# Decoder layer: norm taken behind the projection, chunk order, dots and early loads moved, additions per tile

## The chip, the cores and the metric

The kernel runs on one core of one Trainium2 chip. The metric is the time of one execution in device microseconds; where several runs are made, their median counts.

## The reference

One layer of a decoder. 16 meta tokens and 512 tokens of 1024 numbers are normed and projected by one matrix to queries, keys and values of two attentions (a differential one, and one over 128 keys that an indexer picks), the indexer's own queries and keys, and two gates. Both outputs are projected, gated, added and projected again. Then a feed-forward part picks 128 of 16384 single-neuron experts for each token by product keys, 16 for each of 8 heads.

```
xn = rms_norm(h, mix_norm_gain)
proj = xn @ w_in
aq, ak, av, bq, bk, bv, iq, ik, iw, gate_a, gate_b = split(proj)
aq, ak = rope(rms_norm(aq)), rope(rms_norm(ak))
...
mixed = sigmoid(gate_a) * y_a + sigmoid(gate_b) * y_b
h = h + mixed @ w_out
hn = rms_norm(h, ffn_norm_gain)
...
act = gelu(einsum('thkd,td->thk', u[expert], hn))
h = h + einsum('thk,thkd->td', g * act, v[expert])
```

`rms_norm(x, gain)` is `x * rsqrt(mean(x*x) + eps) * gain`.

## The kernel before, in words

All order is written out by hand: each engine has its own program, and semaphores join them. The engines are PE (matrix products), DVE, ACT and POOL (elementwise work) and SP, which issues most DMAs. Products of full fp32 precision are made of three fp32r products: a matrix is split into a high part (a cast, by ACT) and a low part (the difference, by POOL or DVE), and high x high, high x low and low x high are summed in PSUM.

**Projection** (`project`, lines 203 to 676). x comes in four tiles of 128 tokens, the meta tokens in a fifth of 16 rows. `CHUNKS` (line 62) lists ten chunks of output columns: `ak`, `small` (bk, bv, ik, iw: 200 columns), `av`, `aq`, four gate chunks, `iq`, `bq`, each of 512 columns but for `small`. A chunk is two pieces of four blocks of 128 rows of the weights; a slot is one piece for one token tile, 12 products. So slots 0 to 4 are `ak`'s first piece for tiles 0 to 4, slots 5 to 9 its second. Before that PE transposes each tile (`turn_x`, L616), DVE multiplies the bank by the norm's gain (L386), ACT takes the high part (L530), DVE the low part (L375). The sum of squares of x (L512), its root (L516), the inverse (L196 to L200) and the scaling of x (L369) stand ahead of it. ACT splits the weights (L524) and POOL subtracts (L345); POOL fills `ident`, `tri` and three key tiles at the start (L331 to L341).

The query and key chunks then are normed by head and rotated: ACT squares the bank (L575), DVE reduces it, ACT takes the root (L579), DVE inverts it and rotates in the bank (L484, L415 to L418), PE turns the result (L629), ACT copies it out. A bank is used again six steps (chunk and tile) later, and PE waits for its rotation. DVE builds the rotation tables with the gains and the lambda first (L398 to L409), and ACT's exp for the lambda (L534) stands ahead of its split of the third piece.

**Attention and routing** (`mix_and_route`) follows to about 740 us, and then the **experts' first half**: for each of 128 columns (expert index modulo 128), PE multiplies 128 rows of u, split by ACT (L1319, `uh`) and POOL (L1401, `ul`), by three token tiles (L1161 to L1163); ACT applies GELU (L1326) and SP stores the result to `act_mat` (L951). SP loads u four columns ahead (L947). The fourth token tile (number 3, `GATHERED`) goes another way: its 128 picked rows of u are gathered one a time by POOL (L1409), and DVE makes a dot product of each with the tile (L1586). The columns are staged: in three **turn** stages of 16 columns (30 to 45, 64 to 79, 98 to 113) PE multiplies half a column and then four one-hot matrices of four tokens (L1187) that DVE builds (L1685, L1688), in 32 groups, to lay out the gates; between them are **gaps** (46 to 63, 80 to 97), in which the gates of the tile before are stored (L958), and behind them the **tail** (114 to 127). `dot_plan` lays the 128 dots into these places, `GATHER_AT` each gather two columns behind the dot that frees its buffer.

```
        if i == 3:
            plan += [("gap", i, j, 2 * STARTS[i] + j * 2 * AHEAD[i] // GAP_DOTS) for j in range(GAP_DOTS)]
        plan += [("turn", i, g, 2 * TURNS_AT[i] + g // 2) for g in range(TURNS * TURN_GROUPS) if g % 8 != 7]
```

**The v stage** (`experts`): for each column, gates times activations (L1904) is split (ACT L1895, DVE L1909), v is split (ACT L1878 or L1893, DVE L1906), and PE adds up 18 products for three token tiles in six banks (L1864). SP loads v, gates and activations in pairs of columns; `load_early` issues those of pair 0 and part of pair 1 behind column 124. DVE adds the gathered rows of v for tile 3 (L1922, gathers by POOL L1844). At the end DVE adds the banks to the stream, tile by tile (L1929), and SP stores it (L1834).

Of the kernel before, what the change touches and what calls it, by code (L numbers as in the profile page):

```python
# [61 lines left out]
CHUNKS = ["ak", "small", "av", "aq", "gate", "iq", "gate", "bq", "gate", "gate"]  # L62
# [141 lines left out]
def project(nc, m, d):  # L204
# [6 lines left out]

    xn = placer(nc, m.free2)("xn", [P, 2, D])
# [31 lines left out]
    ms = gap("ms", [P, 8])  # L244

# [11 lines left out]
    xn_ready = nc.alloc_semaphore("xn_ready")  # L257
    xn_turned = nc.alloc_semaphore("xn_turned")
# [17 lines left out]
    N_PIECES = PIECES * len(CHUNKS)  # L276

# [21 lines left out]
    with nc.Block() as block:  # L299
        @block.sync  # L300
        def _(sp):
# [8 lines left out]
            load_weights(0)  # L310
            load_weights(1)
# [17 lines left out]
        def _(pool):  # L329
# [12 lines left out]
            for n in range(N_PIECES):  # L342
                w = width_of(n)
                pool.wait_ge(w_high, n + 1)
                nc.gpsimd.tensor_tensor(wlo[:, n % 3, :, 0:w], wraw[:, n % 3, :, 0:w], whi[n % 2][:, :, 0:w].bitcast(F32),  # L345
                                        ALU.subtract).then_inc(w_low, 1)

        @block.vector
        def _(dve):
# [9 lines left out]
            dve.wait_ge(squared, NT + 1)  # L359
            nc.vector.tensor_scalar(ms[:, 0:NT + 1], sums[:, 0:NT + 1], 1.0 / D, EPS, ALU.mult, ALU.add).then_inc(ms_ready, 1)  # L360
            dve.wait_ge(root_ready, 1)
            inverse_root(nc, step, inv[:, 0:NT + 1], root[:, 0:NT + 1], ms[:, 0:NT + 1])

            def normed(i):
                r = rows_of(i)
                src = m.stream[:, i, :] if i < NT else meta[:]
                if i >= 2:
                    dve.wait_ge(xn_turned, i - 1)
                nc.vector.tensor_scalar(xn[0:r, i % 2], src, inv[0:r, i:i + 1], None, ALU.mult).then_inc(xn_ready, 1)  # L369

# [6 lines left out]
            normed(0)  # L377
            normed(1)
            dve.wait_ge(mix_loaded, 16)
            for i in range(NT + 1):  # L380
                r = rows_of(i)
                dve.wait_ge(xn_turned, i + 1)
# [4 lines left out]
                if i + 2 <= NT:  # L387
                    normed(i + 2)
                dve.wait_ge(gained_x, i + 1)
                low_of(i)  # L390


# [47 lines left out]
            for q, n in enumerate(ROT_STEPS):  # L440
# [12 lines left out]
                if kind == "small":  # L453
# [13 lines left out]
                    if i < NT:  # L467
                        nc.vector.tensor_scalar(m.iw[:, i], x[:, 3 * HEAD:SMALL], IDX_HEADS ** -0.5 * HEAD ** -0.5,
                                                None, ALU.mult)
# [1570 lines left out]
```

## Time and profile before

| | us |
|---|---|
| median of 3 runs | 1881.32 (1880.59 to 1883.3) |
| profiled execution, its own time | 1884.28 |
| its span, first to last instruction | 1882.5 |
| PE busy | 1778.0 (94%) |
| PE weight loads, beside the products | 1483.5 (79%) |
| DVE busy | 1344.6 (71%) |
| ACT busy | 721.2 (38%) |
| POOL busy | 660.8 (35%) |
| mean granted clock of PE | 0.967 |

A busy time is the time in which an engine has an instruction in work. The span holds all instructions of the program; the time of an execution holds some 2 us more. The granted clock is 1.00 at 2.4 GHz and 0.50 at 1.2 GHz. The page cuts the span in 40 slices of 47 us, and gives in tenths how busy each engine is in each; where PE's digit is 9 and its clock is not, or the other way round, is where to look.

### The profile page before, as it was taken

The page shows a single profiled execution, that of the slowest core. Times are in us where ns is not written, and L with a number is a line of the kernel's source. Part 1 is how long each engine was busy: PE and PEld are TensorE (multiplying, and loading weights), DVE is VectorE, ACT ScalarE, POOL GpSimd, SP SyncE. Part 2 cuts the span into 40 slices and gives each one's busy share as a digit, 9 for nine tenths or more (in the row PEclk, how much of TensorE's full clock was granted, in tenths as well). Part 3 has the DMA queues.
Part 4 walks back from the last instruction along what each step waited for, and adds up shares of the span by engine and source line. Part 5 has one row for each costly group of instructions (what it writes and reads, how often), then busy time and mean ns, then how long its engine had stood idle before and what let it go on. Part 6 is the DMA issues. An engine that isn't in the chain of part 4 may idle for free.

```text
span 1882.5 us, 24827 instructions
## 1 busy us (share of the span) xinstructions
PE 1778.0 (94%) x8763; PEld 1483.5 (79%) x8767; DVE 1344.6 (71%) x2706; ACT 721.2 (38%) x1201; POOL 660.8 (35%) x416
## 2 busy tenths in 40 slices
PE   5899998999878989999989998999899999999998
PEld 4788875554555678999989998999788888888886
DVE  6843268465546877979979953992588888888886
ACT  4333334141222232355435533553343343343342
POOL 3234320000000332677676777776322222222220
PEclk9899997999898999999989999999899999999999
DMA  3222202434242662588887899886999999899993
GB/s 126 68 84 95 91 30 105 158 110 152 96 155 90 206 201 84 163 294 282 281 325 261 286 360 406 309 284 208 362 361 334 327 333 333 328 333 332 328 333 118
DMA packets 170192, 429.78 MB, mean 228 GB/s; under 512 B 15328, under 2 KB 66144, under 8 KB 165744
## 3 DMA queue, kind: packets, MB, share of 16 engines
q1 hardware_dynamic: 133056, 294.23, 45.4%
q0 software_dynamic: 36864, 134.23, 19.3%
q8 instruction: 55, 0.90, 0.2%
q14 instruction: 41, 0.34, 0.0%
q10 hardware_dynamic: 176, 0.07, 0.0%
HBM read 384.44 MB, written 44.04 MB: 228 GB/s over the span
## 4 chain that ended last, share of the span: by engine, by line
PE 73%; DVE 6%; DMA 3%; ACT 1%; issue 1%; POOL 1%; DVEq 0%; ACTq 0%
PE psum L1864 28%; PE psum L1161 8%; PE psum L1162 8%; PE psum L1163 8%; PE psum L1103 6%; PE psum L1187 5%; PE psum L1090 3%; PE psum L1011 3%; DMA u<-in_u 2%; PE psum L1059 1%; POOL ul L1401 1%; PE psum L1142 1%; DMA act_mat<-act_w 1%; DVE nmax L1460 1%; DVE hits L1615 1%
## 5 line engine op out<-in xcount | busy, mean ns | idle before, releaser
L1401 POOL TENSOR_TENSOR ul<-u,uh 128x1024 fp32r<-128x1024 f32 x128 | 321.8, 2515 | 532.3 <-ACT uh L1319 531.0
L1161 PE MATMUL psum<-split,uh 128*128 128x384 f32 x1024 | 357.0, 349 | 13.8 <-POOL ul L1401 13.8
L1163 PE MATMUL psum<-split,ul 128*128 128x384 f32 x1024 | 345.1, 337 | 0.0
L1162 PE MATMUL psum<-split,uh 128*128 128x384 f32 x1024 | 345.1, 337 | 0.0
L1844 POOL DMA_INDIRECT v_row<-in_v,gv x128 | 122.3, 956 | 383.5 <-DVE psum L1922 369.9
L1864 PE MATMUL psum<-vl,wh 128*128 128x512 f32 x768 | 240.9, 395 | 0.0
L1161 PEld LDWEIGHTS psum<-split,uh 128*128 128x128 f32 x1024 | 194.6, 190 | 18.0 <-POOL ul L1401 16.3
L1162 PEld LDWEIGHTS psum<-split,uh 128*128 128x128 f32 x1024 | 194.6, 190 | 1.4 <-issue 1.4
L1163 PEld LDWEIGHTS psum<-split,ul 128*128 128x128 f32 x1024 | 194.1, 190 | 0.0
L1864 PEld LDWEIGHTS psum<-vl,wh 128*128 128x128 f32 x768 | 144.9, 189 | 33.9
L1922 DVE SCALAR_TENSOR_TENSOR psum<-v_row,w,psum 128x1024 f32<-128x1024 f32 x127 | 162.8, 1282 | 0.0
L1319 ACT CAST uh<-u 128x1024 fp32r<-128x1024 f32 x128 | 133.6, 1045 | 74.6 <-DMA u<-in_u 74.5
L1326 ACT ACTIVATE act_w<-psum 128x384 f32<-128x384 f32 x128 | 62.9, 491 | 242.6 <-PE psum L1163 231.1
L1891 ACT COPY gate<-stage 128x128 f32 (+1 forms) x126 | 37.6, 299 | 298.8 <-PE psum L1864 286.9
L345 POOL TENSOR_TENSOR wlo<-wraw,whi 128x2048 fp32r<-128x2048 f32 (+1 forms) x20 | 87.3, 4363 | 165.5 <-ACT whi L524 165.5
L658 PE MATMUL psum<-whi,xTh 128*128 128x512 f32 (+1 forms) x344 | 135.6, 394 | 8.7 <-DVE rot L418 4.0
L1904 DVE TENSOR_TENSOR gate<-gate,act_v 128x384 f32<-128x384 f32 x128 | 73.4, 574 | 88.1 <-ACT gate L1877 46.1
L1685 DVE TENSOR_TENSOR hot<-iota,psum 128x1024 f32<-128x1024 f32 x96 | 116.8, 1217 | 26.1 <-PE psum L1175 25.4
L660 PE MATMUL psum<-whi,xTl 128*128 128x512 f32 (+1 forms) x344 | 133.3, 388 | 0.0
L659 PE MATMUL psum<-wlo,xTh 128*128 128x512 f32 (+1 forms) x344 | 132.9, 386 | 0.0
L1586 DVE SCALAR_TENSOR_TENSOR rows_sb<-rows_sb,psum 128x1024 f32<-128x1024 f32 x86 | 103.8, 1215 | 37.7 <-DMA rows_sb<-in_u_rows,tri 37.7
L1864 PE MATMUL psum<-vh_first,wh 128*128 128x512 f32 x384 | 121.9, 398 | 6.7 <-DVE wl L1909 6.7
(291 smaller groups left out, 3376.0 us busy)
## 6 DMA issues: line engine op xcount, KB each, us to landing
u<-in_u SPq DMA_DIRECT2D x128, 512.0 KB, 5.0
v<-in_v SPq DMA_DIRECT2D x64, 1024.0 KB, 5.0
act_mat<-act_w SPq DMA_DIRECT2D x128, 192.0 KB, 5.1
act_v<-act_mat SPq DMA_DIRECT2D x64, 384.0 KB, 6.7
wraw<-in_w_wide SPq DMA_DIRECT2D x18, 1024.0 KB, 5.1
gate_mat<-stage SPq DMA_DIRECT2D x16, 1024.0 KB, 10.1
gate<-gate_mat SPq DMA_DIRECT2D x128, 128.0 KB, 6.1
w_low<-in_w_branch_b SPq DMA_DIRECT2D x8, 1024.0 KB, 5.2
```

The costliest lines, as they stand in the source:

```text
L658: nc.tensor.matmul(ps, xh, wh, start=(part == 0 and k == 0), stop=False)
L659: nc.tensor.matmul(ps, xh, wl, start=False, stop=False)
L660: last = nc.tensor.matmul(ps, xl, wh, start=False, stop=(part == PIECES - 1 and k == PK - 1))
L1161: nc.tensor.matmul(out, high[:, c], split[:, 0:DENSE, 0, c], start=(c == 0), stop=False)
L1162: nc.tensor.matmul(out, high[:, c], split[:, 0:DENSE, 1, c], start=False, stop=False)
L1163: last = nc.tensor.matmul(out, low[:, c], split[:, 0:DENSE, 0, c], start=False, stop=(c == DC - 1))
L1319: nc.scalar.copy(uh[:, n % UH_COLS], u[:, n % U_COLS]).then_inc(s["u_high"], 1)
L1401: nc.gpsimd.tensor_tensor(ul[:, n % U_COLS], u[:, n % U_COLS], uh[:, n % UH_COLS].bitcast(F32), ALU.subtract).then_inc(s["u_low"], 1)
L1685: nc.vector.tensor_tensor(hot[:, b], keys, bcast(turned[:, 0:2, some], 3, N_KEYS), ALU.is_equal).then_inc(s["hot_rows"], 1)
L1844: nc.gpsimd.indirect_dma_start(out=rows_sb[k % V_RING][:], out_offset=None, in_=d.v.rearrange("j i n -> (j i) n"), in_offset=bass.Indirect ...
L1864: mm = nc.tensor.matmul(bank(m, 2 * i + half), lhs, rhs[:, half * 512:(half + 1) * 512], start=first and k == 0 and p == 0, stop=last and ...
L1922: nc.vector.scalar_tensor_tensor(mixed0, rows_sb[n % V_RING][:], m.w0[:, n:n + 1], mixed0, ALU.mult, ALU.add).then_inc(s["mixed"], 1)
```

## The change

The parts, in the order of the program:

- `CHUNKS` has `av` second and `small` third.
- x is transposed and split as it comes (`turn_x` reads the stream, `xn` is gone). The inverse norm of each token, `inv_x`, is worked out behind the split of x, and multiplies the products where they leave PSUM (as `scale` of ACT's instruction, or of a copy), the inverse of each head's norm for the rotated chunks (a new DVE instruction in `head_scale`), and `iw`.
- SP issues x tile 0, the first weights, x tiles 1 and 2, the second weights, x tile 3.
- The first weights are split in two halves; PE waits for each. ACT splits the second weights after the second x tile, POOL's three key memsets stand behind the first weights.
- `GAP_DOTS` is 14 instead of 28; all 32 groups of a turn stage have a dot; the tail has 10 instead of 8.
- `load_early` becomes `load_first` (pair 0, behind column 116) and `load_second` (v and activations of pair 1, behind column 120).
- On ACT the cast of the first `wh` and the GELU of the dots stand ahead of the last two columns.
- PE signals each token tile of the last column by itself, and DVE adds it then.

```diff
-CHUNKS = ["ak", "small", "av", "aq", "gate", "iq", "gate", "bq", "gate", "gate"]
+CHUNKS = ["ak", "av", "small", "aq", "gate", "iq", "gate", "bq", "gate", "gate"]
...
             for i in range(NT):
                 sp.dma_start(m.stream[:, i, :], d.x[i * P:(i + 1) * P, :]).then_inc(x_loaded[i], 16)
-            load_weights(0)
-            load_weights(1)
+                if i in (0, 2):
+                    load_weights(i // 2)
...
-            nc.gpsimd.memset(m.akT[:], 0.0)
-            nc.gpsimd.memset(m.bkT[:], 0.0)
-            nc.gpsimd.memset(m.ikT[:], 0.0).then_inc(keys_zeroed, 1)
             for n in range(N_PIECES):
+                if n == 1:
+                    nc.gpsimd.memset(m.akT[:], 0.0)
...
-                pool.wait_ge(w_high, n + 1)
...
+                for k, chunks in enumerate(HALVES if n == 0 else (slice(0, PK),)):
+                    pool.wait_ge(w_high, parts_before(n) + k + 1)
...
-            def normed(i):
...
-                nc.vector.tensor_scalar(xn[0:r, i % 2], src, inv[0:r, i:i + 1], None, ALU.mult).then_inc(xn_ready, 1)
...
                 low_of(i)
 
+            dve.wait_ge(squared, NT + 1)
+            nc.vector.tensor_scalar(ms_x[:, 0:NT + 1], sums[:, 0:NT + 1], 1.0 / D, EPS, ALU.mult, ALU.add).then_inc(ms_ready, 1)
+            dve.wait_ge(root_ready, 1)
+            inverse_root(nc, step, inv_x[:, 0:NT + 1], root_x[:, 0:NT + 1], ms_x[:, 0:NT + 1])
+            nc.vector.tensor_copy(ms_x[:, 0:NT + 1], inv_x[:, 0:NT + 1]).then_inc(x_inverse, 1)
...
+                if heads == GROUPS:
+                    step(nc.vector.tensor_scalar(inv[0:r, 0:heads], inv[0:r, 0:heads], inv_x[0:r, i:i + 1], None, ALU.mult))
...
+            act.wait_ge(dve_order, 1)
+            split_weights(0)
+            high_of(0)
+            high_of(1)
+            split_weights(1)
+            squares_of(0)
+            squares_of(1)
+            high_of(2)
+            squares_of(2)
+            squares_of(3)
+            high_of(3)
+            squares_of(NT)
+            high_of(NT)
...
                     if q == 0:
                         act.wait_ge(x_low, NT + 1)
+                        act.wait_ge(x_inverse, 1)
...
-                        nc.scalar.activation(raw[0:r, q % 2], ps, ACT.Square).then_inc(evacuated, 1)
+                        nc.scalar.activation(raw[0:r, q % 2], ps, ACT.Square, scale=inv_x[0:r, i:i + 1]
+                                             ).then_inc(evacuated, 1)
...
-                    nc.scalar.copy(m.av[0:r, i], ps).then_inc(evacuated, 1)
+                    nc.scalar.mul(m.av[0:r, i], ps, inv_x[0:r, i:i + 1]).then_inc(evacuated, 1)
...
             def turn_x(i):
...
-                pe.wait_ge(xn_ready, i + 1)
+                pe.wait_ge(x_loaded[i], 16)
...
-                                               xn[0:r, i % 2, c * P:(c + 1) * P], m.ident[0:r, 0:r])
...
+                                               src[:, c * P:(c + 1) * P], m.ident[0:r, 0:r])
...
-                    if i == 0:
-                        pe.wait_ge(w_low, piece + 1)
+                    if i == 0 and slot > 0:
+                        pe.wait_ge(w_low, parts_before(piece) + 1)
...
+                        if slot == 0 and k % (PK // 2) == 0:
+                            pe.wait_ge(w_low, 2 * k // PK + 1)
...
-GAP_DOTS = 28
+GAP_DOTS = 14
...
-        plan += [("turn", i, g, 2 * TURNS_AT[i] + g // 2) for g in range(TURNS * TURN_GROUPS) if g % 8 != 7]
+        plan += [("turn", i, g, 2 * TURNS_AT[i] + g // 2) for g in range(TURNS * TURN_GROUPS)]
...
-                if n == N_KEYS - U_COLS:
-                    late.load_early(sp)
+                if n == 2 * TAIL_AT + 2:
+                    late.load_first(sp)
+                if n == 2 * TAIL_AT + 6:
+                    late.load_second(sp)
...
             late.high_of_v(act, 1)
-            alone(PAIRS - 1, PAIRS)
+            late.high_of_w(act, 0)
             act.wait_ge(s["dotted"], PICKS)
             nc.scalar.activation(dots[:], dots[:], ACT.Gelu).then_inc(s["act0_ready"], 1)
+            alone(PAIRS - 1, PAIRS)
             late.high_parts(act)
...
         load_pair(sp, 0, 0)
+
+    def load_second(sp):
         load_v(sp, 2, 1)
         load_activated(sp, 2, 1)
...
-                mm.then_inc(s["summed"], 1)
+                    if last and k == RING - 1:
+                        mm.then_inc(s["tile_summed"], 1)
+                if not last or k < RING - 1:
+                    mm.then_inc(s["summed"], 1)
...
+    def high_of_w(act, n):
+        act.wait_ge(s["gated"], n + 1)
+        nc.scalar.copy(wh[n][:], gate[n // 2][:, n % 2]).then_inc(s["w_high"], 1)
...
-        dve.wait_ge(s["summed"], N_KEYS)
         for i in range(DENSE):
+            dve.wait_ge(s["tile_summed"], i + 1)
             nc.vector.tensor_tensor(m.stream[:, i, :], m.stream[:, i, :], bank(m, 2 * i, 2),
                                     ALU.add).then_inc(s["added"], 1)
```

**Order.** The first instructions of ACT that work (raw and part are scratch, `whi` the weights' high part, `xTh` that of x). Before:

```order
L512 ACT_TABLE_LOAD
L512 ACTIVATE raw,sums<-meta 16x1024
L512 ACTIVATE raw,sums<-stream 128x1024 x4
L516 ACT_TABLE_LOAD
L516 ACTIVATE root<-ms 128x5
L524 CAST whi_71<-wraw 128x2048
L530 CAST xTh<-raw 128x8x128
L530 CAST xTh<-rot 128x8x128
L530 CAST xTh<-raw 128x8x128
```

And now:

```order
L514 ACT_TABLE_LOAD
L514 CAST whi_71<-wraw 128x1024 x2
L519 CAST xTh<-raw 128x8x128
L519 CAST xTh<-rot 128x8x128
L514 CAST whi_72<-wraw 128x2048
L525 ACTIVATE part,sums<-stream 128x1024 x2
L519 CAST xTh<-raw 128x8x128
L525 ACTIVATE part,sums<-stream 128x1024 x2
L519 CAST xTh<-rot 128x8x128
L525 ACTIVATE part,sums<-meta 16x1024
L519 CAST xTh<-raw 128x8x16
L544 ACT_TABLE_LOAD
```

The squares have moved from ahead of all to between the casts of x, and the second weights stand between tiles 1 and 2.

POOL behind its constants (`wlo` is the weights' low part, `akT`, `bkT` and `ikT` the key tiles). Before:

```order
L338 IOTA iota_i 128x128
L339 MEMSET akT 128x4224
L340 MEMSET bkT 128x1056
L341 MEMSET ikT 128x1056
L345 TENSOR_TENSOR wlo<-wraw,whi_71 128x2048
L345 TENSOR_TENSOR wlo<-wraw,whi_73 128x2048
L345 TENSOR_TENSOR wlo<-wraw,whi_71 128x4x200
```

And now:

```order
L345 IOTA iota_i 128x128
L354 TENSOR_TENSOR wlo<-wraw,whi_71 128x1024 x2
L348 MEMSET akT 128x4224
L349 MEMSET bkT 128x1056
L350 MEMSET ikT 128x1056
L354 TENSOR_TENSOR wlo<-wraw,whi_72 128x2048
L354 TENSOR_TENSOR wlo<-wraw,whi_71 128x2048
```

The memsets stand between the first and the second weights, and the third piece is wide.

SP behind column 116 of the experts' first half, as it is now (L967 loads u, L971 stores activations, L1815 to L1822 load the v stage's first pairs):

```order
L971 DMA act_mat<-act_w 128x384
L1815 DMA v_2622<-in_v 128x2x1024
L1819 DMA gate_2632<-gate_mat 128x2x128 x2
L1822 DMA act_v_2640<-act_mat 128x768
L967 DMA u<-in_u 128x1024
...
L971 DMA act_mat<-act_w 128x384
L1815 DMA v_2623<-in_v 128x2x1024
L1822 DMA act_v_2641<-act_mat 128x768
L967 DMA u<-in_u 128x1024
```

Before, both portions stood together behind column 124:

```order
L951 DMA act_mat<-act_w 128x384 x2
L1792 DMA v_2596<-in_v 128x2x1024
L1796 DMA gate_2606<-gate_mat 128x2x128 x2
L1799 DMA act_v_2614<-act_mat 128x768
L1792 DMA v_2597<-in_v 128x2x1024
L1799 DMA act_v_2615<-act_mat 128x768
L951 DMA act_mat<-act_w 128x384 x3
```

The loads have left the last stores' neighbourhood; the gates of pair 1 stay behind the last column in both.

## Rows read from the trace of the kernel before

**Rows 1.** Waits of PE, 0 to 250 us: us in all, times, longest.
```profile
PE psum L629 <- DVE rot L472: 4.7, 2, 2.6
PE psum L658 <- DVE rot L418: 4.0, 2, 2.4
```

**Rows 2.** DMA issues at 0.7 and 2.7 us: size, us to landing.
```profile
stream<-in_x SPq DMA_DIRECT2D x1, 512.0 KB, 4.3
...
wraw<-in_w_wide SPq DMA_DIRECT2D x1, 1024.0 KB, 8.6
```

**Rows 3.** Timeline: start, duration (us), engine, line, instruction; idle before it.
```profile
2.44 3.61 POOL L339 MEMSET akT<- 128x4224 f32 x1
2.60 3.53 DVE L354 CAST ident_b<-ident 128x128 bf16<-128x128 f32 x1 [1.71 <-POOL iota_i L338]
4.40 1.28 ACT L512 ACT_TABLE_LOAD   x1 [4.40 <-DMA meta<-in_meta_tokens]
13.25 1.88 ACT L524 CAST whi<-wraw 128x2048 fp32r<-128x2048 f32 x1
18.55 1.05 ACT L530 CAST xTh<-raw 128x1024 fp32r<-128x1024 f32 x1 [3.42 <-DVE raw L386]
20.66 1.21 DVE L375 TENSOR_TENSOR xTl<-raw,xTh 128x1024 fp32r<-128x1024 f32 x1
22.02 0.47 PE L658 MATMUL psum<-whi,xTh 128*128 128x512 f32 x1 [3.14 <-DVE xTl L375]
```

**Rows 4.** Windows: PE, PEld, DVE, ACT, POOL busy (count), clock, DMA, GB/s; then timeline.
```profile
42.00:56.00 14.00, 13.88 (x60) 11.28 (x61) 11.43 (x36) 3.63 (x7) 1.98 (x2) 1.00 0.09 28
63.60:66.90 3.30, 3.30 (x15) 3.30 (x16) 2.76 (x9) 1.84 (x4) 0.00 (x0) 0.50 0.02 5
...
37.39 4.68 POOL L345 TENSOR_TENSOR wlo<-wraw,whi 128x2048 fp32r<-128x2048 f32 x1 [17.20 <-ACT whi L524]
37.56 4.70 DVE L401 TENSOR_TENSOR sin_ak<-sin,gains 128x160 f32<-128x160 f32 x1
52.26 0.69 DVE L433 TENSOR_REDUCE ms<-raw 128x8 f32<-128x512 f32 x1
56.72 0.69 DVE L418 TENSOR_TENSOR rot<-psum,part 128x512 f32<-128x512 f32 x1
115.31 0.39 PE L658 MATMUL psum<-whi,xTh 128*128 128x512 f32 x1
```

**Rows 5.** Windows of the third gap and of the tail.
```profile
1093.00:1180.00 87.00, 79.90 (x434) 77.69 (x433) 30.05 (x50) 26.27 (x35) 66.00 (x44) 0.96 1.01 396
1276.00:1334.00 58.00, 58.00 (x336) 57.79 (x334) 7.20 (x12) 20.65 (x30) 35.40 (x19) 1.00 0.69 223
```

**Rows 6.** Second turn stage: window, two DVE rows, a row of the chain.
```profile
1000.00:1092.00 92.00, 92.00 (x619) 91.60 (x618) 90.71 (x123) 54.20 (x61) 65.33 (x45) 1.00 0.86 280
...
1046.09 0.08 DVE L1586 DVE_READ_ACCUMULATOR rows_sb<-rows_sb,psum 128x1 f32 x1
1049.08 0.08 DVE L1586 DVE_READ_ACCUMULATOR rows_sb<-rows_sb,psum 128x1 f32 x1
1044.49 0.89 PE psum L1187 x8
```

**Rows 7.** Before the v stage: chain, timeline of SP, PE, ACT, window after.
```profile
1326.35 12.59 DMA act_mat<-act_w
1339.90 0.95 SPq L1796 DMA_DIRECT2D gate<-gate_mat  x2
1340.84 0.77 PE L1864 MATMUL psum<-vh_first,wh 128*128 128x512 f32 x1 [6.72 <-DVE wl L1909]
1346.65 0.30 ACT L1891 COPY gate<-stage 128x128 f32<-128x128 f32 x1 [3.43 <-DMA gate<-gate_mat]
...
1340.00:1347.00 7.00, 6.16 (x15) 4.84 (x16) 5.31 (x7) 0.96 (x4) 1.94 (x2) 0.50 1.04 405
```

**Rows 8.** Timeline of the end, DVE.
```profile
1875.77 3.48 DVE L1929 TENSOR_TENSOR stream<-stream,psum 128x1024 f32<-128x1024 f32 x3 [11.20 <-PE psum L1864]
```

More of the change, by code:

```diff
@@ L276, in project, with parts_before @@
     N_PIECES = PIECES * len(CHUNKS)
+    SQUARED = (0, 1, 2, 3, NT)
+    HALVES = (slice(0, PK // 2), slice(PK // 2, PK))
+    def parts_before(piece):
+        return piece + (piece > 0)
     def width_of(piece):
@@ L428, in rotate, with head_scale @@
                 return nc.vector.tensor_tensor(out, a, b, ALU.add)
-            def head_scale(sq, heads, k):
+            def head_scale(sq, heads, k, i):
                 r = sq.shape[0]
@@ L505, in _ @@
             act.dma_start(m.mix_gain[:], d.mix_gain).then_inc(mix_loaded, 16)
-            act.wait_ge(dve_order, 1)
-            for k, i in enumerate([NT] + list(range(NT))):
-                r = rows_of(i)
-                act.wait_ge(x_loaded[i], 16)
-                src = m.stream[:, i, :] if i < NT else meta[:]
-                nc.scalar.activation(raw[0:r].rearrange("p a b -> p (a b)"), src, ACT.Square,
-                                     accum_out=sums[0:r, i:i + 1]).then_inc(squared, 1)
-                act.wait_ge(squared, k + 1)
-            act.wait_ge(ms_ready, 1)
-            nc.scalar.activation(root[:, 0:NT + 1], ms[:, 0:NT + 1], ACT.Sqrt).then_inc(root_ready, 1)
             def split_weights(n):
@@ L523, in split_weights, with high_of @@
                 w = width_of(n)
-                nc.scalar.copy(whi[n % 2][:, :, 0:w], wraw[:, n % 3, :, 0:w]).then_inc(w_high, 1)
-            split_weights(0)
-            for i in range(NT + 1):
+                for chunks in HALVES if n == 0 else (slice(0, PK),):
+                    nc.scalar.copy(whi[n % 2][:, chunks, 0:w], wraw[:, n % 3, chunks, 0:w]).then_inc(w_high, 1)
+            def high_of(i):
                 lo = columns_of(i)
@@ L1779, in experts @@
     gathered = [nc.alloc_semaphore(f"v_gathered{k}") for k in range(V_RING)]
[L1780 removed]
+    names = "v_high v_low gate_kept gated w_high w_low summed tile_summed mixed added stored".split()
     s = s | {n: nc.alloc_semaphore(n) for n in names}
@@ L1893, in body @@
                     nc.scalar.copy(vh[k % HIGH_RING], v[k // 2][:, k % 2]).then_inc(s["v_high"], 1)
-                act.wait_ge(s["gated"], n + 1)
-                nc.scalar.copy(wh[k % HIGH_RING][:], gate[k // 2][:, k % 2]).then_inc(s["w_high"], 1)
+                if not first or k >= 1:
+                    act.wait_ge(s["gated"], n + 1)
+                    nc.scalar.copy(wh[k % HIGH_RING][:], gate[k // 2][:, k % 2]).then_inc(s["w_high"], 1)
         rounds(act, body)
```

66 lines of the change are left out of this document (35 added, 31 removed).

## Prediction

> **What bounds the kernel now.** I read the page first (which engine is busy in which slice), then the waits of PE, and then, for each stretch in which PE waits, the timeline, the windows with the granted clock, and the chain of waits. PE is busy for 94% of the span and heads the chain, so two things alone are worth anything: time in which PE stands still, and time in which it runs at 1.2 instead of 2.4 GHz after it stood still. Other engines' work beside a busy PE is priced at nothing.
>
> In the projection PE's first product starts at 22.02 us [rows 3]. Behind it PE waits 4.0 us for banks that DVE must rotate first and 4.7 us at the turns of the narrow chunk [rows 1]; such a wait is often followed by a stretch at clock 0.50 [rows 4]. In the third gap (columns 80 to 97) PE is busy 79.90 of 87.00 us while the DMA engines are at 1.01 of their time [rows 5]. Before the v stage PE stands for 6.72 us, and the 7 us that follow go at clock 0.50 [rows 7]. At the end DVE adds three tiles one after the other [rows 8]. The rest of PE's idle time lies in the attention stage, which is not touched.
>
> **Start of the projection.** The norm leaves the path: the squares, a root, the inverse and the scaling of x. The first x tile lands 4.3 us after an issue at about 0.8, so at 5.1; the first weights land 8.6 us after an issue at about 2.6, at 11.2, behind four x tiles [rows 2]. So 2560 KB came in 6.1 us, 2.4 us for 1024 KB. In the new order the weights come behind one tile: 5.1 + 2.4 = 7.5. ACT then loads its table (1.28) and casts the weights in halves (1.88 in all): 9.8 and 10.8. Only then comes the high part of x (1.05): 11.8 [rows 3]. POOL subtracts the first half meanwhile (half of 4.68, to 12.3). DVE's low part of x (1.21) has both inputs in SBUF and cannot run beside that: such an instruction of 128x160 took 4.70 us where POOL subtracted for 4.68 [rows 3, 4]. That gives 13.5 for PE's first product, 8.5 us earlier.
>
> The lead is not kept whole. Each tile passes DVE (gain, of the same width as the low part: 1.2), ACT 1.05, DVE 1.21 in series, 4 us with the hand-overs, against 2.8 us of products (60 matmuls in 14.00 us, 12 a slot) and a turn [rows 3, 4]; and ACT now has the second weights (1.88) and the squares between these casts. POOL does its memsets behind the first weights (to about 21) and then the second weights, which holds DVE's low part of tile 2 until 26. I get product slots 1, 2 and 3 at 19.5, 27 and 31, and slot 5 (second weights) at about 36.6 where it was 42.1. The ends are 32.4 (tile 2 gets in ahead of POOL) and 38.
>
> The low part of tile 1 meets a memset. The nearest row has a CAST of 128 columns held for 3.53 us beside a memset of 3.61 [rows 3], so I take it as held: slot 1 a microsecond later, and tile 2 sure to be behind POOL's subtraction. The Trainium skill (SBUF — State Buffer, "Who interferes with whom") says that a DVE instruction with two SBUF inputs contends with a GpSimd instruction that reads SBUF, not with one that only writes it. By it this memset holds nothing, tile 2 comes to its low part at 21.8 with POOL's subtraction due at 21.3, and the early end of 32.4 is half a microsecond away; the sum would then be up to 4 us better. No run shows the case yet.
>
> **Chunk order.** Rotating one ak tile takes DVE from 52.26 to 57.41, 5.2 us [rows 4], plus one new instruction of 0.2: 5.4. After ak came the narrow chunk, whose slots take 1.1 to 1.4 us, and PE caught up with DVE; now ten av slots of 2.8 us come first. The rotations start no earlier than tables and lambda: x is split at 31.5, root and inverse take 3, the tables 5 (estimates from the widths), and then the third weights, wide now, hold DVE behind POOL until 46.5. The first rotation is done at 51, the next at 56.6, 63 (once more behind POOL), 68.7 and 74; PE wants the first at 50.5, the third at 60 and the fourth at 66 and waits 0.6, 3 and 2.4 us. Later the narrow chunk's first rotation meets POOL's subtraction for aq (4.6 us) and PE waits 4 us at its turn. So 10 us of waits stand where 8.7 stood: they move, they do not go. With two or three slow stretches (each 3.4 us at half rate, 1.7 lost), the first aq product comes at about 107.5 instead of 115.3 [rows 4], and four small turns (0.5) are still to come: **7 us** for the whole stage, between 3 and 12. After that the order is as before and DVE has time, so the gain is kept.
>
> **Dots.** In the third gap 18 columns want 18 x 704 KB (u tile and store), eight gate stores of 1024 KB and 28 gathers of 512 KB: 36.0 MB, 91 us at the row's 396 GB/s; the stretch took 87 [rows 5]. The floor is PE's: 14 tail columns took 58.00 us, 4.14 each [rows 5], so 75 us for 18. With 14 gathers it is 28.7 MB or 72.5 us, just under the floor. In the 16 columns with stores the demand is 397 GB/s, right at what the row delivers, so I leave 2 us of waits: 87 - 75 - 2 = **10 us**, between 6 and 12. The removed dots go into turn groups that had none (12) and into the tail (2). A group with a dot takes DVE 2.99 us; it takes PE half a column (2.07) and the eight small products (0.89), 2.96 [rows 5, 6]. Groups without a dot let DVE catch up. Some 72 of the 96 groups by 0.03: **2 us** lost (the first eight groups of each turn have dots from the start and already go at DVE's pace), between 0 and 3. The tail's dots are done long before PE needs them.
>
> **Early loads of v.** The chain before the v stage is a store of act_mat that takes 12.59 us (it shares the DMA engines with 3072 KB of early loads and six gathers of v rows), ACT's last GELU, one cast and one subtraction [rows 7]. The loads now go out after columns 116 and 120, where DMA moves only 223 GB/s [rows 5]; behind the first of them the queue is longer by 1664 KB, 4.2 us, and u tiles are asked for four columns (16.6 us) ahead, so nothing waits there. The cast of w and the GELU of the dots stand ahead of the last pair, beside the last columns. Against gathers alone I take 6 to 7 us for the store (estimate), so it lands before the last column ends at 1334.1; then GELU 0.5 and PE starts at 1334.8 instead of 1340.84: 6.0 us. After so short a stop the clock should stay up; 6.1 us at 0.50 had cost 3.1. Late next are the gates of pair 1, still asked for only after the last column. They were asked for at 1339.90 and landed at 1346.65 [rows 7]; from 1335.1 they land at 1341.8, copy, split and product take 3 (estimate), and PE wants them at 1334.8 + 8.3 = 1343.1, so 1.5 is lost again: **7.6 us**, between 4 and 9.5.
>
> **End.** DVE's three additions (3.48 us from 1875.77) become one behind the last matmul (1.2) [rows 8]: **2.3 us**, give or take 0.2.
>
> **Sum.** 7 + 10 - 2 + 7.6 + 2.3 = 24.9. Against the profiled execution (span 1882.5, time 1884.28) that is 1857.6 and 1859.4. The median of the runs lies 3.0 below that execution, so **1856**. A measurement of this kernel tells about 0.2% (3.8 us) from no change.
>
> **Rivals.** *The projection stays bound by DVE.* POOL's subtractions hit the fourth and fifth rotation as well and the clock falls after each wait: the 7 shrinks to 1, 1862. For it: three of my waits are already conflicts of DVE and POOL. Against: PE starts 8.5 us sooner.
>
> *The gap stays full.* 397 GB/s are wanted where 396 came; u tiles go on coming late through eight stores, and 10 becomes 4: 1862. For it: DMA at 1.01 [rows 5]. Against: half of the gathers are gone.
>
> *Slower, by the dots in the turn groups.* DVE has no spare time left in 96 groups. If each dot waits d for its row, PE loses 96 d; from d = 0.26 the whole gain is gone, at 0.35 it is 1890. Against: with seven dots in eight groups DVE's instructions follow each other without a pause, and DMA is at 0.86 there [rows 6].
>
> *The early loads do not do what they say.* The six gathers (3 MB) are the store's real neighbours; if it still takes over 10 us, PE starts at 1337 or later and the clock drops: 7.6 becomes 3, 1860.5.
>
> *A better start.* No hold at the memset, and tile 2 ahead of POOL: 4 us more, 1852.
>
> **Chances.** Forecast, each term near its value: 0.50 (1850 to 1862 by itself). Projection alone poor 0.13, gap alone poor 0.12, early loads poor 0.08, better start 0.10, nothing left of the gain (several poor, within 3.8 us) 0.03, slower by the dots 0.04. The range of 1847 to 1866 leaves out the slow end and the sums of two poor cases. Faster by over 0.2%: 0.93, within 0.03, slower 0.04.
>
> **What would show it.** First product at 13 to 16 us, slot 5 at 33 to 38, the first aq product at 104 to 111, and DVE instructions of 3 to 5 us beside POOL's weight subtractions. In the gap 76 to 80 us for 18 columns; in the turns groups at 2.99. At the v stage one wait under 1.5 us and a clock that stays at 1.00, then a short wait at pair 1; one addition after the last matmul. I am wrong if the first aq product comes after 112, if the gap still takes over 83 us, or if the v stage starts more than 2 us after the last column.

## The result, and the profile after

| | before | after |
|---|---|---|
| median of the runs side by side | 1880.95 us (6 runs, 1876.89 to 1883.74) | 1865.89 us (6 runs, 1860.17 to 1871.45) |
| ratio | | 0.9912, 95% interval 0.9895 to 0.9929 |
| profiled execution, its own time | 1884.28 | 1860.17 |
| its span | 1882.5 | 1858.4 |
| PE busy | 1778.0 (94%) | 1769.8 (95%) |
| mean granted clock of PE | 0.967 | 0.976 |

The change is faster by 0.9%, 17 us by the ratio, where 24.9 were forecast (1856 us). The median lies within the range of 1847 to 1866, at its very end. The profiled execution is the fastest of the six; two more sets of runs of the same kernel (e1, e9) gave medians of 1860.07 and 1864.6 and ratios of 0.9883 and 0.9896, so the gain is about 19 us. That the profiled execution lies so near the forecast of 1859.4 for it is luck.

The start of the page: digits are tenths in each of 40 slices.

```profile
PE   7989998899878999999989999999899999999999
...
PEclk9999997999998999999999999999999999999999
```

Most of what is left of idle PE and low clock lies in the slices of the attention stage (7, 8 and 11 to 13 of the 40), as before; the rest is the start (slices 1 and 3), column 58 (slice 21) and the start of the v stage (slice 29). I read the stages from the timeline of PE: the start of the first product at slot 40 (the third slot of the first gate chunk), at columns 9, 80, 98 and 127 of the experts' first half, and at column 4 of the v stage. The times between these marks, in all profiled executions of this study:

| kernel | to slot 40 | to col. 9 | to 80 | gap, to 98 | to 127 | to v col. 4 | to the end |
|---|---|---|---|---|---|---|---|
| before | 143.5 | 570.2 | 379.0 | 87.4 | 149.7 | 30.5 | 522.1 |
| **after** | 138.0 | 564.7 | 380.5 | 75.6 | 150.6 | 29.3 | 519.6 |
| e1, change again | 139.3 | 564.1 | 380.3 | 76.5 | 150.5 | 26.6 | 519.6 |
| e2, gathers held | 140.3 | 569.7 | 379.8 | 76.0 | 151.4 | 21.7 | 520.9 |
| e3, low parts in four | 134.5 | 570.5 | 379.9 | 79.2 | 150.4 | 29.7 | 519.6 |
| e4, projection as before | 145.3 | 569.9 | 379.5 | 79.9 | 150.5 | 29.2 | 519.7 |
| e5, dots as before | 141.0 | 564.6 | 377.5 | 85.4 | 149.5 | 29.9 | 519.6 |
| e6, loads late | 139.1 | 560.9 | 380.1 | 75.9 | 150.2 | 30.8 | 519.6 |
| e7, narrow second | 139.0 | 570.2 | 380.1 | 75.8 | 150.2 | 29.5 | 519.6 |
| e8, three edits | 134.7 | 570.2 | 375.7 | 75.8 | 150.5 | 21.7 | 523.6 |
| e9, change a third time | 140.8 | 568.3 | 380.6 | 77.5 | 151.1 | 29.8 | 519.6 |
| e10, narrow second again | 138.7 | 567.4 | 379.7 | 76.0 | 150.3 | 29.6 | 519.6 |
| e11, six ahead | 134.9 | 570.4 | 375.7 | 76.1 | 150.3 | 22.2 | 519.6 |

The first two rows differ by 24.1 us: 5.5 in the projection, 5.5 in the attention stage, 11.8 in the gap, 1.2 at the v stage, 2.5 at the end, less 2.4 in turns, at column 58 and in the tail. None of the instructions of the attention stage was changed; how much of its 5.5 us the change brings all the same stays open (e1, e4, e7).

**The projection.** The waits of PE from 0 to 250 us, which answer to [rows 1]:

```profile
PE psum L634 <- DMA stream<-in_x: 7.1, 2, 5.4
PE psum L647 <- DVE rot L473: 6.6, 3, 4.2
PE psum L678 <- DVE xTl L372: 6.2, 2, 3.4
PE psum L678 <- DVE rot L417: 3.3, 2, 2.8
```

The timeline of POOL, DVE and PE in the projection, rows of the start (as [rows 3]) and of the narrow chunk:

```profile
13.78 0.79 PE L678 MATMUL psum<-whi,xTh 128*128 128x512 f32 x1 [2.73 <-DVE xTl L372]
15.90 3.62 POOL L348 MEMSET akT<- 128x4224 f32 x1
16.04 1.23 DVE L372 TENSOR_TENSOR xTl<-rot,xTh 128x1024 fp32r<-128x1024 f32 x1 [1.18 <-ACT xTh L519]
21.33 4.55 POOL L354 TENSOR_TENSOR wlo<-wraw,whi 128x2048 fp32r<-128x2048 f32 x1
22.43 4.53 DVE L372 TENSOR_TENSOR xTl<-raw,xTh 128x1024 fp32r<-128x1024 f32 x1 [1.24 <-ACT xTh L519]
...
94.60 4.57 POOL L354 TENSOR_TENSOR wlo<-wraw,whi 128x2048 fp32r<-128x2048 f32 x1 [5.82 <-ACT whi L514]
94.87 4.38 DVE L460 TENSOR_TENSOR part<-raw 128x64 f32<-128x64 f32 x1 [21.65 <-ACT raw L586]
106.33 4.49 DVE L424 TENSOR_TENSOR part<-raw,icos 128x32 f32<-128x32 f32 x1
120.24 4.54 DVE L467 COPY bv<-raw 128x64 f32<-128x64 f32 x1
```

PE starts at 13.78 instead of 22.02. The low part of tile 1 takes its 1.23 us beside the memset; that of tile 2 takes 4.53 us beside POOL's subtraction. The three last rows are small DVE instructions of the narrow chunk, each held while POOL splits a wide piece (at 94.60, 106.18 and 120.14); the first of them makes PE's wait of 4.2 us, which ends at 103.4, just ahead of the first aq product.

**The gap and the tail**, windows as in [rows 5]:

```profile
1083.00:1158.80 75.80, 75.66 (x438) 75.30 (x438) 17.13 (x30) 26.57 (x36) 57.42 (x33) 1.00 1.00 381
1254.90:1313.70 58.80, 58.76 (x339) 58.16 (x337) 17.46 (x29) 22.10 (x32) 42.02 (x24) 1.00 0.81 279
```

PE does not stop in the third gap any more, at 381 GB/s.

**The start of the v stage**: the chain of waits (as in [rows 7]), the timeline of ACT and DVE at pair 1, and the window around it:

```profile
1313.92 0.50 ACT act_w L1348
1314.81 0.43 SPq L1819
1315.29 9.88 DMA gate<-gate_mat
...
1325.19 0.30 ACT L1923 COPY gate<-stage 128x128 f32<-128x128 f32 x1 [10.38 <-DMA gate<-gate_mat]
1327.61 0.55 DVE L1942 TENSOR_TENSOR wl<-gate,wh 128x384 fp32r<-128x384 f32 x1
...
1323.00:1332.00 9.00, 3.78 (x10) 2.95 (x10) 6.09 (x8) 4.46 (x8) 1.00 (x1) 0.66 1.05 392
```

The first product comes at 1314.5, 5.1 us after column 127's instead of 11.0. Then the gates of pair 1, asked for at 1314.8, take till 1325.2, and PE stands 5.2 us at the second pair and comes back at the low clock. At the end DVE's additions follow PE tile by tile (the row holds all three), and the last product is 4.6 us from the end where it was 7.1 [rows 8]:

```profile
1851.42 3.94 DVE L1962 TENSOR_TENSOR stream<-stream,psum 128x1024 f32<-128x1024 f32 x3 [8.48 <-PE psum L1889]
```

### The profile page after: what moved, and what is told of

It reads as the page before. It is cut to its first block, busy times and chain, and to the rows that moved or that the text cites. A ratio compares the mean times of both kernels' runs of the same rounds, so it can differ in the third digit from the quotient of the medians.

```text
span 1858.4 us, 24842 instructions
## 1 busy us (share of the span) xinstructions
PE 1769.8 (95%) x8767; PEld 1472.3 (79%) x8767; DVE 1339.7 (72%) x2715; ACT 723.5 (39%) x1202; POOL 661.8 (36%) x417
## 4 chain that ended last, share of the span: by engine, by line
PE 76%; DVE 5%; DMA 1%; ACT 1%; issue 1%; POOL 1%; SPq 0%; DVEq 0%; ACTq 0%
PE psum L1889 28%; PE psum L1183 9%; PE psum L1185 9%; PE psum L1184 9%; PE psum L1125 6%; PE psum L1209 5%; PE psum L1112 3%; PE psum L1033 3%; PE psum L1081 2%; PE psum L1164 1%; PE psum L1059 1%; DVE nmax L1483 1%; DMA gate<-gate_mat 1%; DVE score L1455 1%; DMA u<-in_u 0%
## 5 line engine op out<-in xcount | busy, mean ns | idle before, releaser
L1183 PEld LDWEIGHTS psum<-split,uh 128*128 128x128 f32 x1024 | 193.7, 189 | 10.5 <-POOL ul L1424 8.8
L354 POOL TENSOR_TENSOR wlo<-wraw,whi 128x2048 fp32r<-128x2048 f32 (+2 forms) x21 | 87.7, 4180 | 160.1 <-ACT whi L514 160.1
L1708 DVE TENSOR_TENSOR hot<-iota,psum 128x1024 f32<-128x1024 f32 x96 | 116.9, 1217 | 36.6 <-PE psum L1197 36.6
L1364 ACT COPY stage<-psum 128x512 f32<-128x512 f32 x96 | 106.2, 1106 | 67.9 <-PE psum L1209 67.8
L1889 PE MATMUL psum<-vh_second,wh 128*128 128x512 f32 x384 | 120.5, 395 | 5.2 <-DVE wl L1942 5.2
```

Source lines behind the costliest of these rows:

```text
L1183: nc.tensor.matmul(out, high[:, c], split[:, 0:DENSE, 0, c], start=(c == 0), stop=False)
L1708: nc.vector.tensor_tensor(hot[:, b], keys, bcast(turned[:, 0:2, some], 3, N_KEYS), ALU.is_equal).then_inc(s["hot_rows"], 1)
L1889: mm = nc.tensor.matmul(bank(m, 2 * i + half), lhs, rhs[:, half * 512:(half + 1) * 512], start=first and k == 0 and p == 0, stop=last and ...
```

## The experiments

Each kernel was timed beside the kernel before on one chip; medians of different sets are compared by their ratios to it. e1 to e4 were timed together, so were e5 to e8, and e9 to e11.

**e1, the change again.** No edit.

> The changed kernel itself once more. Its profiled execution was 5.7 us below its median, and the attention stage (281 to 702 us), which the change does not touch, was 5.75 us shorter than before, with 68.3 us at granted clock 0.50 in it where the kernel before had 78.5. Theory A (the clock's stretches fall differently in every execution): attention takes anything from 421 to 433 us this time, and its time follows half of its half-clock time to within 1 us; projection (first aq product at 103 to 106), third gap (75 to 77 us) and first v product (within 1 us of the last column) repeat to within 1 us. Rival B (the change really shortens attention): attention takes 421 to 423 us again. Median 1863 to 1868 by both.

Median 1860.07 us (5 runs), ratio 0.9883 (0.9865 to 0.9901). Projection 1.3 us longer, gap and v start as expected, pair 1 came 1.8 us sooner (its v column 2 at 12.0 us behind the first product instead of 13.8). The attention stage gave the same 432 us as in the profiled execution of after, as rival B wants, and the median is 3 us below the 1863 to 1868 expected. What speaks against a B that gives the same gain each time are the others: after, e1, e2, e5, e6 and e9 have the same instructions up to column 9, and took 432.5, 431.9, 437.5, 432.5, 428.7 and 436.1 us (mean 433.2) from the projection's last slot to column 9; before took 438.3. That all six lie below it leaves room for a B on the average, to which e4 and e7 come back. The windows of after and of e2:

```profile
270.20:702.70 432.50, 385.64 (x1588) 246.98 (x1587) 281.26 (x889) 131.28 (x328) 31.26 (x12) 0.92 0.41 139
```

```profile
272.50:710.00 437.50, 394.73 (x1586) 251.81 (x1588) 284.56 (x891) 131.39 (x328) 31.91 (x12) 0.90 0.41 138
```

PE does the same work and is busy 9 us longer, at a mean clock of 0.90 instead of 0.92. The time does not simply follow the half-clock time as I had written: before and e2 had 78.5 and 88.7 us of it in 438.3 and 437.5 us. Where PE waits anyway, a slow stretch costs nothing.

**e2, gathers held.**

```diff
-            if k == V_RING - 2:
+            if k == V_RING - 4:
                 pool.wait_ge(s["hidden"], N_KEYS)
+                pool.wait_ge(loaded[1], LOADS)
```

> The change, but POOL issues 4 instead of 6 gathers of v rows ahead of the last column, and the next only when the v stage's second pair has landed. Theory (the gates of pair 1 took 9.9 us because the gathers had 78% of the DMA engines' time beside them): they land within 5 us of their issue, PE's 5.2 us wait at pair 1 falls to 1.5 or less and the 6.8 us at clock 0.50 behind it go: 6 to 8 us faster than the change, so 1858 to 1860. Rival (the gates are slow by themselves, 256 descriptors of 512 B behind the last stores): they take 8 us or more again, the wait stays over 3 us, and the time is within 2 us of the change.

The timeline of ACT at pair 1, and the use of the DMA queues while the gates were under way, in e2 (1322.5 to 1325.7 us):

```profile
1325.69 0.30 ACT L1924 COPY gate<-stage 128x128 f32<-128x128 f32 x1 [3.20 <-DMA gate<-gate_mat]
...
q1 hardware_dynamic: 758, 0.61, 73.0%
q0 software_dynamic: 30, 0.08, 6.1%
```

And in after, 1314 to 1320 us (q0 is POOL's queue with the gathers, q1 holds SP's transfers; the last number is the share of the DMA engines' time):

```profile
q0 software_dynamic: 525, 1.90, 78.1%
q1 hardware_dynamic: 558, 0.49, 23.7%
```

The gates, asked for at 1322.5, were there 3.2 us later instead of 10.4, and both the wait at pair 1 and the slow stretch are gone: 21.7 us from column 127 to v column 4, 7.6 less than after. The theory holds for the mechanism. In the time little of it is seen: median 1860.41 (4 runs), ratio 0.9865 (0.9850 to 0.9880) against 0.9883 and its interval of e1. The 6 to 8 us expected did not come. The trace gives 2.1 of the 7.6 us back, 0.8 in the tail and 1.3 in the rest of the v stage, where PE has a new wait of 1.0 us 26 us in.

**e3, low parts in four.**

```diff
-                for k, chunks in enumerate(HALVES if n == 0 else (slice(0, PK),)):
-                    pool.wait_ge(w_high, parts_before(n) + k + 1)
+                for k, chunks in enumerate(HALVES if n == 0 else QUARTERS):
+                    pool.wait_ge(w_high, parts_before(n) + (k if n == 0 else 0) + 1)
...
-                        pe.wait_ge(w_low, parts_before(piece) + 1)
+                        pe.wait_ge(w_low, lows_before(piece) + PK)
```

> The change, but POOL subtracts each piece of the weights but the first in four instructions of 128x512 instead of one of 128x2048. Theory (a DVE instruction with both inputs in SBUF is held until POOL's instruction ends, and gets in between two): the holds of 3.3 to 4.5 us on DVE become 1.2 us or less, PE's waits in the projection from 50 to 140 us shrink from 10.3 us to 3 to 5, one slow clock stretch less: slot 40 at 131 to 134 instead of 138.0, 4 to 7 us faster, 1859 to 1862. Rival (the hold lasts as long as POOL works, whatever the number of instructions): holds of 3 to 5 us stay and so does the time, within 2 us.

POOL's and DVE's timeline of e3, at the second weights, at the first ak rotation and at the narrow chunk:

```profile
20.90 6.00 POOL L359 TENSOR_TENSOR wlo<-wraw,whi 128x512 fp32r<-128x512 f32 x4
21.66 1.60 DVE L377 TENSOR_TENSOR xTl<-raw,xTh 128x1024 fp32r<-128x1024 f32 x1 [1.24 <-ACT xTh L524]
...
38.04 5.07 POOL L359 TENSOR_TENSOR wlo<-wraw,whi 128x512 fp32r<-128x512 f32 x4 [11.13 <-ACT whi L519]
39.36 1.26 DVE L438 TENSOR_SCALAR ms<-ms 128x8 f32<-128x8 f32 x1
41.91 1.22 DVE L198 TENSOR_TENSOR root<-root,ms 128x8 f32<-128x8 f32 x1
...
92.92 1.09 DVE L465 TENSOR_TENSOR part<-raw 128x64 f32<-128x64 f32 x1 [23.22 <-ACT raw L591]
```

A hold lasts until POOL's instruction ends: four short ones let DVE in between, at 5.07 us for POOL instead of 4.6. Of DVE's small instructions none takes more than 1.3 us any more, but now several in a row are held: at 103 to 108 us four take 1.18, 1.30, 1.17 and 1.21 us, where beside the whole piece one took 4.49. PE's waits from 50 to 140 us fell only from 10.3 to 8.4 us, not to 3 to 5. Most of the gain is at the start: the low part of tile 2 takes 1.60 us instead of 4.53, and slot 5 starts at 33.7 instead of 36.3. Slot 40 comes at 134.5, half a microsecond behind the band, 3.5 us sooner than in after and 5.2 sooner than the mean of the six executions of the whole-piece kernels (after, e1, e2, e5, e6, e9: 139.75).

The median, 1861.21 (ratio 0.9874, 0.9858 to 0.9889), can't tell it from e1: the gain of the projection is not in the time. In the profiled execution the attention stage, from the projection's last slot to column 9, took 438.5 us, 5.3 above the mean of the six. The same stage took 438.3 and 438.5 in e8 and e11, which have this projection too, each time with 81.9 us at granted clock 0.50. The gap took 79.2 us here, with a wait of 2.2 us and a slow stretch.

**e4, projection as before.** `project` and `CHUNKS` are those of the kernel before.

> The change with the projection of before (norm ahead of the products, narrow chunk second): dots, early loads and additions as in the change. By the two traces the projection's part is 5.2 us (slot 40 at 143.5 instead of 138.0), so this is 4 to 7 us slower than the change: 1870 to 1873. By rival B (attention gains through the projection as well) it is 10 to 12 slower: 1876 to 1878.

Median 1874.76, ratio 0.9939 (0.9925 to 0.9952). Beside e1 (0.9883), with which it was timed, that is 10.5 us slower by the ratios, as B says; against the other two sets of the change (0.9896 and 0.9912) it is 8 and 5 us. Slot 40 at 145.3 is 5.5 us behind the mean of 139.75, so more may be lost than the projection's own part. Its attention stage took 438.0 us, above all six of the change. The medians do not settle between the theory and B.

**e5, dots as before.** `GAP_DOTS = 28`, and `if g % 8 != 7` put back in `dot_plan`.

> The change with the dots as before (28 in the third gap, none in every eighth group, 8 in the tail). Theory (the third gap is bound by what the DMA engines deliver, and half of its gathers are half of its excess): columns 80 to 97 take 86 to 89 us instead of 76 to 80, a turn stage 0.6 us less, so 8 to 11 us slower than the change. Rival (the gap was slow in the execution before by luck of the clock): 80 to 83 us, 3 to 5 slower.

Median 1867.8, ratio 0.9925 (0.9905 to 0.9945). The window of columns 80 to 97:

```profile
1083.10:1168.50 85.40, 79.26 (x439) 76.48 (x437) 30.33 (x50) 26.30 (x35) 65.23 (x43) 0.98 1.01 400
```

The gap takes 85.4 us, 9.8 more than after, half a microsecond under the theory's band and above the rival's 80 to 83; the columns before it, with two turn stages and column 58, take 3.0 less (380.5 to 377.5), and those behind it, with the third, 1.1 less. Net that is about 6 us by the trace and 2 to 8 by the ratios, less than the 8 to 11 expected of the whole, since the turn stages give 1.7 us back and the stretch with column 58 took 2.1 us less in this execution. Moving the dots is worth this much.

**e6, loads late.** Both portions behind column 124 again, ACT's order as in the change.

> The change with both early portions of v behind column 124 again, the order on ACT as in the change. The forecast put 7.6 us on the early loads; the traces give 1.2 (30.5 to 29.3 us from column 127 to the first product of column 4) and 3.8 us in a second execution, because the gates of pair 1 come late in place of the last store. Theory (one wait took the place of the other): PE's first v product comes 9 to 11 us after column 127's first instead of 5.1, the wait at pair 1 is under 2 us, and the whole is 1 to 5 us slower than the change. Rival (the early loads are worth the 7.6 us forecast): 7 to 9 us slower.

Median 1862.72, ratio 0.9896 (0.9882 to 0.9911), the same as the change. The waits of PE, and the chain of waits:

```profile
PE psum L1888 <- ACT act_w L1347: 5.8, 1, 5.8
PE psum L1888 <- DVE wl L1941: 1.8, 1, 1.8
```

```profile
1302.80 12.89 DMA act_mat<-act_w
1317.13 8.37 DMA gate<-gate_mat
```

With the loads late the store takes 12.89 us and PE waits 5.8 us ahead of the first product and 1.8 at pair 1; with the loads early it waits 0.8 and 5.2. 30.8 us against 29.3, 26.6 and 29.8 for the change: one wait took the place of the other, as the theory says. The 1 to 5 us that it wanted in the time can't be seen in the medians. The rival, the forecast's own 7.6 us, falls.

**e7, narrow second, and e10, the same again.** `CHUNKS` as before.

> The change with the narrow chunk second again. Theory (av's ten wide slots hide some of DVE's rotations of ak, but most of it comes back at the narrow chunk's turns): slot 40 comes at 139 to 143 instead of 138 to 139.3, so 1 to 4 us slower than the change. Rival (the order only moves the waits): slot 40 within 1 us of the change's; a second rival (the order is worth the whole lead): slot 40 at 143 or later.

> e7 again beside the change. Its trace had slot 40 at 139.0 (the change 138.0 to 141.0), yet its median was 1869.0. Theory (the order of the chunks only moves waits; e7's slow attention stage of 438.3 us was the clock's luck): the profiled attention stage differs from e7's, slot 40 at 138 to 141, and the median is within 3 us of e9's. Rival (the order does more: it leaves attention in a state in which the clock falls oftener): attention 437 to 439 us again and a median 4 us or more above e9's.

Slot 40 came at 139.0 and 138.7, within the change's 138.0 to 141.0, so in the projection the order only moves the waits (in e7 4.5 us for banks and 3.5 at turns, in after 3.3 and 6.6). The attention stages were 438.3 and 435.5 us, so e7's was no fixed state. But both medians are high: they are 1869.03 (ratio 0.9925, 0.9912 to 0.9938) and 1868.35 (0.9928, 0.9915 to 0.9941), the second 3.8 us above e9's: more than the theory's 3 and less than the rival's 4. If the chunk order is worth some 3 to 5 us outside the projection, the traces show one place for them: the four executions with the narrow chunk second (before, e4, e7, e10) took 438.3, 438.0, 438.3 and 435.5 us in the attention stage, 437.5 on the average, against 433.2 of the six with av second. All these kernels run the same instructions there. Four and six executions that overlap do not prove it, and how the order would bear on a later stage is shown by nothing here.

**e8, three edits.** e2 and e3, and the gathers at column 58 spread:

```diff
-GATHER_AT = [FIRST_GATHERS] * U_RING + [min(DOTS[k][3] + 2, N_KEYS) for k in range(PICKS - U_RING)]
+GATHER_AT = [FIRST_GATHERS] * U_RING + [min(DOTS[k][3] + 2 + (DOTS[k][0] == "chosen") * max(DOTS[k][2] - 1, 0), N_KEYS)
+                                        for k in range(PICKS - U_RING)]
```

> The change with three edits: v gathers held until pair 1 has landed (e2), low parts of the weights in four instructions (e3), and the eight gathers that POOL issues in one go ahead of column 58 spread: two there, then one a column. Theory: slot 40 at 133 to 136, PE's wait of 7.6 us at column 58 under 2.5 and the clock stretch behind it gone (together 6 to 9 us), no wait at pair 1 (3 to 6 us): 1845 to 1851, against 1860 to 1866 of the change. Rival for the spread (the wait at column 58 comes from DVE's work on the picks beside POOL's subtractions, not from the gathers): it stays over 5 us.

Median 1853.41 (5 runs, 1851.51 to 1854.24), ratio 0.9841 (0.9829 to 0.9854). POOL's timeline at column 58, in after (the first and the last of eight gathers, then the late subtractions) and in e8:

```profile
943.74 0.95 POOL L1432 DMA_INDIRECT rows_sb<-in_u_rows,tri  x1
...
954.19 2.28 POOL L1432 DMA_INDIRECT rows_sb<-in_u_rows,tri  x1 [0.93 <-DVE rows_sb L1609]
956.49 11.10 POOL L1424 TENSOR_TENSOR ul<-u,uh 128x1024 fp32r<-128x1024 f32 x3
```

```profile
946.15 0.95 POOL L1438 DMA_INDIRECT rows_sb<-in_u_rows,tri  x1
947.41 0.94 POOL L1438 DMA_INDIRECT rows_sb<-in_u_rows,tri  x1 [0.30 <-issue]
948.37 2.40 POOL L1430 TENSOR_TENSOR ul<-u,uh 128x1024 fp32r<-128x1024 f32 x1
950.92 0.95 POOL L1438 DMA_INDIRECT abqT<-in_u_rows,tri  x1 [0.16 <-issue]
```

The wait of 7.6 us at column 58 and its slow stretch are gone; three waits for `ul` of 2.9 us in all and one of 1.9 for `hot` come later, and 4.8 us remain as gain (380.5 to 375.7). The time is 2.4 us above what I expected. In this execution the gathers held back in the v stage came with a wait of 2.2 us and a slow stretch of their own: 523.6 us from v column 4 to the end, 4 more than any kernel that gathers as the change does. That does not explain the median, since e11 is rid of both and no faster; the attention stage of 438.3 us, 5 above the mean of the change, may.

**e9, the change a third time.**

> The changed kernel a third time, beside e10 and e11 on one chip. Five profiled executions with the same instructions up to column 57 took 428.8 to 437.5 us from the end of the projection to column 9, by where the clock's slow stretches fell, so only medians of many runs compare kernels here. By both earlier sessions together: median 1860 to 1866, ratio to before 0.988 to 0.991.

Median 1864.6 (6 runs, 1856.3 to 1869.56), ratio 0.9896 (0.9877 to 0.9916), as expected. (In e5, one of the five executions named there, the dots already differ from column 33 on; the stretch that is compared ends at column 9 and is the same.) All 17 runs of the change lie between 1856.3 and 1871.45, with their median at 1864.4.

**e11, six ahead.** e8 with `V_RING - 2` in place of `V_RING - 4`.

> The three edits of e8, but with six gathers of v rows ahead of the last column as in the change, and only those behind them held until pair 1 has landed. In e8 the v stage had a new wait of 2.2 us and a slow stretch some 34 us in, since the gathers started late met the loads. Theory (what slowed the gates were the gathers already under way): gates land in 7 us or more and PE waits 2 to 4 us at pair 1 again; no later wait; the time within 2 us of e8's 1853.4. Rival (what slowed them were the four issued beside them): gates in under 5.5 us, no wait at pair 1 and none later: 1849 to 1852.

ACT's timeline at pair 1:

```profile
1318.14 0.30 ACT L1930 COPY gate<-stage 128x128 f32<-128x128 f32 x1 [5.52 <-DMA gate<-gate_mat]
```

The gates were there 5.5 us after their issue at 1312.6, PE came to pair 1 8.9 us behind the first product with a wait of 0.4, where e2 and e8 took 8.4 without one, and no later wait came (519.6 us to the end). So in the change, where the gates took 10.4 us, the four gathers that POOL issued beside them did most of the harm, 4.9 us; six ahead of them instead of four cost the 2.3 us between 3.2 and 5.5. The median is 1854.1 (1851.07 to 1854.82), ratio 0.9844 (0.9831 to 0.9857), the same as e8's and not the 1849 to 1852 that I gave the rival, though its span of 1849.3 was the shortest of the study.

## Why the prediction was right, and where it was not

- **Projection, 7 forecast.** 5.5 by the two profiled executions, 4.7 by the mean of six new (139.75) and two old (143.5, 145.3) ones. The forecast's marks stood: first product 13.78 (13.5), slot 5 at 36.3 (36.6), slots 1 and 2 at 19.7 and 27.0. The choice at the memset was the wrong one: I took the low part of tile 1 as held, and it ran in 1.23 us. The Trainium skill (SBUF — State Buffer, "Who interferes with whom") had said so, and the trace agrees with it; the early end that hung on it did not come, since PE transposed tile 2 only behind slot 0 (at 18.90 us; the products of that slot came 0.43 us apart, those of slot 1 0.23), and tile 2 reached DVE's low part 1.1 us behind the start of POOL's subtraction. The first aq product came at 103.6, sooner than 107.5 (104.7 to 106.5 in e1, e2, e5, e6 and e9). What failed is the 0.5 us for all that was to come behind it: the ten slots to slot 40 took 34.4 us where they had taken 28.2, with 2.8 us of waits, a slow stretch and the turns of the narrow chunk among them. So 11.7 us of lead became 5.5.
- **Attention, nothing forecast.** 5.5 us came in the profiled execution, with 68.3 us at granted clock 0.50 where there had been 78.5. With it the profiled time (1860.17) seems to hit the forecast of 1859.4; the medians show that it did not. I had put the stage at nothing because its instructions stay as they were; e3, e7 and e10 suggest that the projection ahead of it bears on it by some 4 to 5 us either way, and this is not settled.
- **Third gap, 10 forecast.** 11.8 by the traces, 9.8 in e5. 381 GB/s were enough; the 2 us left for waits were mostly not needed: of eleven executions with 14 dots nine took 75.6 to 77.5 us, and e3 and e4, each with one wait of 2.2 or 2.3 us and a slow stretch, 79.2 and 79.9.
- **Turns, -2 forecast.** Each turn stage took 0.5 us more (95.5 to 96.1 for the third), 1.6 in all.
- **Junction and early loads, 7.6 forecast: the step that failed.** The sum there said that the gates of pair 1 would land 6.75 us after their issue, as before, "so 1.5 is lost again". They took 10.4 by the same measure (1314.81 to 1325.19), since four gathers went out beside them, from 0.7 us ahead to 3.1 us behind. Before, two of these four had gone out 4 us and more ahead, while PE still stood, and the third came 2.6 us behind, kept waiting by a late DVE. The first product came 5.9 us sooner, as forecast, and 4.7 were given back at pair 1: 1.2 is left (3.9 and 0.7 in e1 and e9). e6 shows the early loads to be worth nothing that the medians can tell, e2 and e11 show in the traces what stood in the way.
- **End, 2.3 forecast.** 2.5.

With 7.6 replaced by 1.9 (the mean of three) and 7 by 4.7, the sum of 24.9 becomes 17, and 11.8 for the gap instead of 10 makes it 19, the gain of the medians. The match is not exact enough to say that the attention stage gave nothing: the gain is 17 to 22 us in the three sets, and the first terms rest on few traces. The median of 1865.89 is inside the range by 0.1 us; its 9.9 us above the forecast are the junction and the projection, 8 us by this sum, with the rest within the spread of the runs. The rival "the early loads do not do what they say" named the right term but the wrong neighbour: it had the store late, and the store was in time.

## What to carry to other kernels

When a wait goes, look at what the engine that is now early sets going: POOL's gathers started in time with the very load that came next on the path, and took the DMA engines from it. In the traces, holding back four transfers that nobody needs yet was worth more there (7.6 us in e2) than asking for the data early (1.9). Look also at the stages behind the one that got faster: the 5 us that e3 gains in the projection are not in its median, and its attention stage was 5 us longer. Cut the long instructions of an engine that holds up a busy one (e3), and spread a burst of issues on an engine that also computes (e8): with both, and the gathers held, the kernel runs in 1853.4 us (0.9841 of before, against 0.9883 to 0.9912 for the change).

## What the runs showed of the hardware

- The same instructions took 428.7 to 437.5 us in the attention stage in six executions, with 61.4 to 88.7 us of it at granted clock 0.50. The three executions behind e3's projection (e3, e8, e11) took 438.3 to 438.5 us there, each with 81.9 us at 0.50. A single pair of profiles can't tell a few microseconds in such a stage; the spread of runs of the change, 15 us, is of this size.
- Two loads of 128 KB took 3.2 us where four gathers of 512 KB had gone out ahead of them, the last 5.2 us before (e2); 5.5 us behind six, the last 2.7 us before (e11); and 10.4 us behind six with four more beside them, the first 0.7 us ahead (after).
- A DVE instruction of 128x32 took 4.49 us beside a POOL instruction with two SBUF inputs, and the same one 1.18 when POOL's was cut in four, with three of the next four at 1.17 to 1.30; a two-input DVE instruction beside a POOL memset took its normal 1.23.
